# A hybrid decoder step: the turns of q and k placed among retention's phases, and two orders changed on VectorE

## The reference, cut to what matters

```
# stick-breaking attention, a block of queries
z    = (q . k) * d**-0.5
mask = k_pos < q_pos
lm   = where(mask, log_sigmoid(-z), 0)
la   = log_sigmoid(z) + (reverse cumsum of lm over keys) - lm
a    = where(mask, exp(la), 0);   o = a @ v

# retention, a chunk of 128 tokens
att = (q k^T) * inner_decay
o   = att v + (q s) * q_decay
s   = s * chunk_decay + (k * k_decay)^T v
```

## Time and profile before

| | value |
|---|---|
| median of the runs | 1003.06 us |
| profiled execution, its own time | 1003.46 us |
| its span in the profile | 1001.8 us |
| PE busy | 926.3 us (92%) |
| PE weight loads busy | 500.6 us (50%) |
| DVE busy | 477.1 us (48%) |
| ACT busy | 291.1 us (29%) |
| GpSimd busy | 231.7 us (23%) |

### The profile page before, as it was taken

How to read it: one execution, slowest core, us unless ns; L and a number is a source line. 1 busy time by engine, 2 the same in 40 slices (tenths; PEclk the granted TensorE clock), 3 DMA queues, 4 the chain that set the end, 5 groups by cost and what they waited for, 6 DMA issues and landing times.

```text
span 1001.8 us, 15841 instructions
## 1 busy us (share of the span) xinstructions
PE 926.3 (92%) x5202; PEld 500.6 (50%) x5202; DVE 477.1 (48%) x971; ACT 291.1 (29%) x710; POOL 231.7 (23%) x321
## 2 busy tenths in 40 slices
PE   6999999999877978999999999998889898899998
PEld 3544444444444543445465676565544444565444
DVE  1247777879234433112114343724666777556211
ACT  5111111112533334023001010424555556445100
POOL 0000232300123311052243333000443444233000
PEclk9999999999989989999999999999899999999999
DMA  9233666573234327695143132130112132132211
GB/s 346 74 141 118 219 229 227 184 243 71 76 98 138 115 92 223 270 203 186 32 138 121 49 127 55 54 86 11 40 56 64 50 100 94 30 92 71 87 43 43
DMA packets 86070, 117.59 MB, mean 117 GB/s; under 512 B 21006, under 2 KB 49886, under 8 KB 85678
## 3 DMA queue, kind: packets, MB, share of 16 engines
q1 hardware_dynamic: 66432, 80.96, 25.1%
q0 software_dynamic: 9920, 27.31, 9.5%
q10 hardware_dynamic: 9648, 8.41, 2.6%
HBM read 108.68 MB, written 11.36 MB: 120 GB/s over the span
## 4 chain that ended last, share of the span: by engine, by line
PE 86%; DVE 6%; ACT 5%; DMA 2%; issue 1%; SPq 0%; ACTq 0%; DVEq 0%
PE ps L732 25%; PE ps L985 11%; PE ps L991 6%; PE ps L1278 6%; PE ps L1008 4%; PE ps L741 3%; PE ps L1159 3%; PE ps L1170 3%; PE ps L1047 3%; PE ps L928 3%; PE ps L1235 2%; PE ps L908 2%; PE ps L880 2%; PE ps L1025 1%; DVE work L1982 1%
## 5 line engine op out<-in xcount | busy, mean ns | idle before, releaser
L732 PE MATMUL ps<-wring,arena 128*128 128x512 f32 x448 | 197.8, 600 | 1.5 <-issue 1.5
L732 PEld LDWEIGHTS ps<-wring,arena 128*128 128x128 f32 x448 | 85.0, 192 | 105.7 <-issue 105.6
L680 POOL TENSOR_TENSOR z<-z,work 128x1024 f32<-128x1024 f32 (+1 forms) x64 | 80.2, 1252 | 200.8 <-DVE work L1990 200.1
L985 PE MATMUL ps<-wring,z 128*128 128x512 f32 (+2 forms) x320 | 108.4, 494 | 0.0
L1501 ACT ACTIVATE z<-ps,work 128x512 f32<-128x512 f32 (+3 forms) x128 | 66.4, 526 | 71.1 <-DVE work L1982 58.7
L1333 ACT ACTIVATE z<-ps 128x512 f32<-128x512 f32 (+1 forms) x64 | 27.4, 433 | 181.8 <-PE ps L732 147.6
L985 PEld LDWEIGHTS ps<-wring,z 128*128 128x128 f32 x320 | 55.4, 192 | 44.5 <-issue 42.9
L358 POOL DMA_DIRECT2D arena<-cache_sb_k x64 | 34.4, 537 | 165.5 <-DVE work L1618 141.9
L1830 DVE TENSOR_TENSOR arena<-ps,consts 128x512 f32<-128x512 f32 x32 | 30.3, 1022 | 84.0 <-PE ps L1025 84.0
L1512 ACT ACTIVATE arena<-ps 128x512 f32<-128x512 f32 (+3 forms) x128 | 48.9, 438 | 31.2 <-PE ps L1159 31.2
L1982 DVE TENSOR_REDUCE work<-ps 128x1 f32<-128x512 f32 (+3 forms) x128 | 56.9, 486 | 2.2
(11 more groups left out here) (315 smaller groups left out, 1290.7 us busy)
## 6 DMA issues: line engine op xcount, KB each, us to landing
wring<-w_in SPq DMA_DIRECT2D x12, 2048.0 KB, 9.6
arena<-cache_sb_k POOLq DMA_DIRECT2D x64, 256.0 KB, 3.0
arena<-cache_sb_v SPq DMA_DIRECT2D x64, 256.0 KB, 3.4
wring<-w_out SPq DMA_DIRECT2D x3, 2048.0 KB, 7.9
arena<-cache_sel_k SPq DMA_DIRECT2D x64, 64.0 KB, 1.8
consts<-cache_sel_v SPq DMA_DIRECT2D x64, 64.0 KB, 1.8
consts<-aux SPq DMA_DIRECT2D x1, 2299.5 KB, 16.0
xres<-x_prompt SPq DMA_DIRECT2D x4, 512.0 KB, 8.8
```

What stands on the lines that cost most here:

```text
L680: nc.gpsimd.tensor_tensor(P_u(n), P_u(n), bc(coef(n).unsqueeze(2), [P, 2, (NT - n % NT) * P]), ALU.mult).then_inc(n_scaled, 1)
L732: mm = pe.matmul(ps[:, t, 0:width], stat, mov, start=(k == 0), stop=(k == KT - 1))
L985: mm = pe.matmul(ps[:, bank, at:at + w], normed1(k, t), wring[:, slot, k, lo:lo + w], start=(k == 0), stop=(k == KT - 1))
```

## The change

The item list goes. Steps are numbered 0 to 15 and step n uses bank pair n mod 2, so the scores alternate strictly. A turn no longer takes a place in that alternation. The first turn goes into banks 0 and 1 during the last input projection, and DVE copies it as before. The three others are issued at the second step of a pair (n = 1, 5, 9), in banks 4 and 5, which belong to retention: after the tails, PE waits until retention has read these banks, turns, does `values` of the step before and the pages, then waits until the copies are made and only then does retention's phase of that step. ACT makes these copies, after `weights` of the step.

On DVE, the softplus of step n + 1 comes right after `masked` of step n, then `mix`, and then retention's part. On GpSimd, iteration n does the tail sums of step n and no longer those of step n + 1. On ACT, `tail_of` of step 0 comes before the exponential of the sample scores.

```diff
 # PE
-                def front(r):
-                    kind, i, s = sb_items[r]
-                    lo, _ = sb_banks(r)
-                    if r >= 2:
-                        before = sb_items[r - 2][0]
-                        pe.wait_ge(sb_T if before == "turn" else sb_a, sb_count(before, r - 2))
...
+                def sb_turn(i, bank):
+                    for w in range(2):
+                        for t in range(NT):
+                            col = (SQ, SK)[w] * HW + i * P
+                            mm = pe.transpose(ps[:, bank + w, t * P:(t + 1) * P], z[:, t, col:col + P], ident)
+                    mm.then_inc(sb_turned, 1)
+                def front(n):
+                    i, s = SB_STEPS[n]
+                    lo, _ = sb_banks(n)
+                    pe.wait_ge(sb_a, n - 1) if n >= 2 else pe.wait_ge(bank_free, 5 + 5 * RG + NT)
+                    pe.wait_ge(sb_T, 2 * i + 2)
...
+                for n in range(NSTEP):
+                    i, j = n // NT, n % NT
+                    turning = j == 1 and i + 1 < NHP
+                    tails(n)
+                    if n == 0:
+                        rs_sums()
+                    if turning:
+                        pe.wait_ge(*((ret_T, 2), (ret_attm, 4), (ret_S, 4))[i])
+                        sb_turn(i + 1, 4)
+                    else:
+                        retention(n)
+                    if n:
+                        values(n - 1)
+                    sample_pages(n)
+                    if turning:
+                        pe.wait_ge(sb_T, 2 * i + 4)
+                        retention(n)
+                    if n + 2 < NSTEP:
+                        front(n + 2)
 # ACT
-                act.wait_ge(ds_lasum, 1)
-                nc.scalar.activation(zs, zs, ACT.Exp).then_inc(ds_a, 1)
...
+                def sb_copies(i, bank):
+                    act.wait_ge(sb_turned, i + 1)
+                    act.wait_ge(sb_z, NT * (i - 1)) if i > 1 else None
+                    nc.scalar.activation(qT_s(i), ps[:, bank, :], ACT.Copy, scale=SCALE).then_inc(sb_T, 1)
+                    nc.scalar.activation(kT_s(i), ps[:, bank + 1, :], ACT.Copy).then_inc(sb_T, 1)
+                tail_of(0)
+                act.wait_ge(ds_lasum, 1)
+                nc.scalar.activation(zs, zs, ACT.Exp).then_inc(ds_a, 1)
                 tail_of(1)
+                for n in range(NSTEP):
+                    i, j = n // NT, n % NT
+                    weights(n)
+                    if j == 1 and i + 1 < NHP:
+                        sb_copies(i + 1, 4)
+                    retention(n)
+                    if n + 2 < NSTEP:
+                        tail_of(n + 2)
 # DVE
-                    if step:
-                        masked(r)
-                        retention(n)
-                    if r + 2 < NITEM:
-                        softplus(r + 2)
-                    if step and n >= NT and n % NT == 0:
-                        mix(n // NT - 1)
+                    masked(n)
+                    if n + 1 < NSTEP:
+                        softplus(n + 1)
+                    if n >= NT and n % NT == 0:
+                        mix(n // NT - 1)
+                    retention(n)
 # GpSimd
-                    if n + 1 < NHP * NT:
-                        tail_sums(n + 1)
+                    tail_sums(n)
```

More of the change, by code:

```diff
@@ L435, in build, with sb_banks @@
             PTURN_STEPS = {41: 0, 42: 1, 43: 2}
[L437 to L454, removed]
+            SB_STEPS = [(i, s) for i in range(NHP) for s in reversed(range(NT))]
+            NSTEP = len(SB_STEPS)
+            def sb_banks(n):
+                return 2 * (n % 2), 2 * (n % 2) + 2
             @block.sync
@@ L648, in _ @@
                 pool.wait_ge(bank_free, 5 + 5 * NCHUNK0)
-                for n in range(NHP * NT):
-                    if n + 1 < NHP * NT:
-                        tail_sums(n + 1)
+                for n in range(NSTEP):
+                    tail_sums(n)
                     if n < 3 * NT and n % 3 == 0:
@@ L874, in tails @@
-                def tails(r):
-                    _, i, s = sb_items[r]
-                    n, (lo, _), N = sb_step(r), sb_banks(r), (NT - s) * P
+                def sb_turn(i, bank):
[9 more added lines that the diff above has]
+                    pe.wait_ge(sb_T, 2 * i + 2)
+                    for u in range(2):
+                        mm = pe.matmul(ps[:, lo + u, 0:(NT - s) * P], kT_s(i, halves(u))[:, s * P:(s + 1) * P],
+                                       qT_s(i, halves(u))[:, s * P:SEQ], start=True, stop=True)
+                    mm.then_inc(sb_z, 1)
@@ L878, in tails @@
+                def tails(n):
+                    i, s = SB_STEPS[n]
+                    (lo, _), N = sb_banks(n), (NT - s) * P
                     pe.wait_ge(sb_sp, n + 1)
@@ L888, in tails, with values @@
                     mm.then_inc(sb_la, 1)
-                def values(r):
-                    _, i, s = sb_items[r]
-                    pe.wait_ge(sb_a, sb_step(r) + 1)
+                def values(n):
+                    i, s = SB_STEPS[n]
+                    pe.wait_ge(sb_a, n + 1)
                     if s == NT - 1:
@@ L917, in _ @@
                         ds_sums()
-                        front(0)
+                        pe.wait_ge(bank_free, 5 + 5 * RG + 2)
+                        sb_turn(0, 0)
                 project_rows(RG, RG % 2, xnT_ready, 0)
+                front(0)
                 front(1)
@@ L930, in out0_tile @@
                             mm.then_inc(mm_done, 1)
-                done = None
-                for r in range(NITEM):
-                    step = sb_items[r][0] == "step"
-                    if step:
[L936 to L943, removed]
-                    if r + 2 < NITEM:
-                        front(r + 2)
+                for n in range(NSTEP):
[17 more added lines that the diff above has]
+                        front(n + 2)
                 pe.wait_ge(w_loaded[0], 16 * 5)
                 out0_tile(0, range(KT - 1))
-                values(done)
+                values(NSTEP - 1)
                 out0_tile(1, range(KT - 1))
@@ L1392, in retention, with tail_of @@
                         rsqrt(stats[0:NB, 40:48], DH, gn_rstd, NT + 1)
-                def tail_of(r):
-                    _, i, s = sb_items[r]
-                    n, (lo, hi) = sb_step(r), sb_banks(r)
+                def tail_of(n):
+                    i, s = SB_STEPS[n]
+                    lo, hi = sb_banks(n)
                     dst = ln_s(n, s)
@@ L1401, in tail_of, with weights @@
                     softplus_tail(ps[:, lo:hi, 0:(NT - s) * P], dst, sb_ln)
-                def weights(r):
-                    _, i, s = sb_items[r]
-                    n, (lo, hi) = sb_step(r), sb_banks(r)
+                def weights(n):
+                    i, s = SB_STEPS[n]
+                    lo, hi = sb_banks(n)
                     act.wait_ge(sb_masked, n + 1)
@@ L1409, in weights @@
                     nc.scalar.activation(a_s(s), ps[:, lo:hi, 0:(NT - s) * P], ACT.Exp).then_inc(sb_a, 1)
-                tail_of(1)
[L1412 to L1417, removed]
+                def sb_copies(i, bank):
[6 more added lines that the diff above has]
+                nc.scalar.activation(zs, zs, ACT.Exp).then_inc(ds_a, 1)
+                tail_of(1)
+                for n in range(NSTEP):
+                    i, j = n // NT, n % NT
[5 more added lines that the diff above has]
+                        tail_of(n + 2)
                 act.wait_ge(mix_turned, NT + 1)
@@ L1733, in retention, with softplus @@
                         rows_gate()
[L1735 to L1745, removed]
+                def softplus(n):
+                    i, s = SB_STEPS[n]
+                    lo, hi = sb_banks(n)
+                    N = (NT - s) * P
                     dve.wait_ge(sb_ln, n + 1)
@@ L1748, in softplus, with masked @@
                     TT(sp_s(s)[:, :, 0:P], sp_s(s)[:, :, 0:P], bc(cst("strict").unsqueeze(1), [P, 2, P]), ALU.mult).then_inc(sb_sp, 1)
-                def masked(r):
-                    lo, hi = sb_banks(r)
-                    dve.wait_ge(sb_la, sb_step(r) + 1)
+                def masked(n):
+                    lo, hi = sb_banks(n)
+                    dve.wait_ge(sb_la, n + 1)
                     TT(ps[:, lo:hi, 0:P], ps[:, lo:hi, 0:P], bc(cst("strict_neg").unsqueeze(1), [P, 2, P]), ALU.add).then_inc(sb_masked, 1)
@@ L1764, in own_columns @@
                     TT(om[:, b * HW:(b + 1) * HW], ps[:, 7, :], cst("own_head"), ALU.mult).then_inc(ds_om, 1)
[L1766 to L1771, removed]
-                        own_columns(n // 2 - 1)
-                    if step:
-                        masked(r)
-                        retention(n)
-                    if r + 2 < NITEM:
-                        softplus(r + 2)
-                    if step and n >= NT and n % NT == 0:
+                dve.wait_ge(sb_turned, 1)
```

(11 more changed lines are left out.)

## The result

The changed kernel takes 976.71 us, the median of 4 runs (974.5 to 979.01), against 1003.34 for the kernel before: a ratio of 0.9733 (95% interval 0.971 to 0.9757). I had forecast 979.6, within 970 to 989. The profiled execution took 977.28 us with a span of 975.6; before it was 1003.46, so 26.2 us went where 23.9 were forecast.

What follows compares the result with a forecast made beforehand. PE's order of work and its idle places were taken as the bound. Terms -14.4 - 5.3 - 7.6 - 0.6 + 2.7 + 1.3 = -23.9 us took 1003.46 to 979.6 us, range 970 to 989.

Steps and rivals of the forecast that it cites:

- Scores two steps ahead, -14.4: Stick-breaking steps: scores issued two steps ahead cover the chain before the tails, so PE's waits there go, -14.4 us.
- The three stalls: PE's idle times of 4.79, 4.80 and 4.80 us before the tails of a pair's widest step, forecast to go.
- My margin of 0.3 us: Narrowest case, second pair: 5.2 us of PE work against a 4.92 us chain; lateness beyond 0.3 us costs PE in full.
- VectorE's order, -5.3: On DVE, mask ahead of the next softplus and mix ahead of retention end the values matmul's waits for the mix, -5.3 us.
- The clock, -7.6 and +1.3: PE's half-speed work behind five stops goes, -7.6 us; page waits may cause one more slow stretch, +1.3 us.
- The second term: One more 2.5 us stretch at half speed after page waits, +1.3 us, with bounds 0 and 9.3.
- the rival with five falls: The clock falls at page waits, five times 1.85 us instead of one of 1.3: +8.0, 987.6 us; chance 0.07.
- The first step, -0.6: On ACT, step 0's softplus goes ahead of the exponential of the samples, which stood on the chain, -0.6 us.
- Copies and GpSimd, 0: ACT's copies of turned q and k stay hidden; GpSimd's sums come some 2 us before they are needed; cost 0.
- The page ring, +2.7: Four V-page buffers reload late: page waits 16.4 us (turning steps 5.4, opening 5.0), +2.7 us against before.
- The second count: A check of the changed stretch from PE's busy time: 97.7 us of work, 119.1 us instead of 143.9, -24.8 us.
- my slower rival: Tails, mask and softplus form a closed cycle, engines working in series: +6.1 us, 1009.6 us; chance 0.03.

Runs made afterwards that it cites:

- e2: The kernel before with VectorE's new order alone, turns left where they were; 997.08 us, ratio 0.9939.
- e1: The changed kernel with VectorE's old order (mask, retention's part, softplus of step n + 2, then mix); 991.79 us, ratio 0.9887.
- e7: The changed kernel with the mix behind retention's part on VectorE, the mask still ahead of the next softplus; 976.26 us, ratio 0.9731.
- e8: The changed kernel with the mask of step n + 1 behind the softplus of step n + 2, the mix still ahead of retention's part; 986.41 us.
- e3: The changed kernel with the three copies of turned q and k made by VectorE in place of ScalarE; 976.57 us, ratio 0.9747.
- e10: The changed kernel with GpSimd's sums of tails one step ahead of its retention jobs, as before; 976.56 us, ratio 0.9742.
- e4: The changed kernel with seven page buffers in place of four and the page loads written out one by one; 965.35 us, ratio 0.9629.
- e5: The changed kernel with its four page buffers but the page loads written out one by one, a control; 978.24 us, ratio 0.9751.

## Why the prediction was right, step by step

*Scores two steps ahead, -14.4.* Right. The three stalls are gone; they stay in e2, where only VectorE's order is changed, and are gone in e1, where it is not. So the placement removes them. My margin of 0.3 us held.

*VectorE's order, -5.3.* Right in the trace: no values matmul waits for the mix. The reason was half right. I put the mix "behind both", the mask of step n+1 and the softplus of n+2; in the order before it stands behind that softplus and ahead of that mask. e7 and e8 show that this softplus is what counts, and that the mix may stand behind retention.

*The clock, -7.6 and +1.3.* The first is right in place, since one low stretch is left, the one at the start; but it was too small. The rows that I halved end before the clock is back. Taken up to where it is back, the five stretches are these (kernel before, columns as above):

```profile
287.70:292.50 4.80, 4.80 (x9) 2.67 (x10) 0.68 (x2) 0.00 (x0) 0.00 (x0) 0.50 0.00 0
323.50:326.60 3.10, 3.10 (x4) 1.48 (x5) 0.68 (x2) 0.00 (x0) 0.00 (x0) 0.50 0.00 0
343.90:347.10 3.20, 3.20 (x16) 1.17 (x17) 0.76 (x2) 1.88 (x5) 2.73 (x4) 0.50 0.01 3
359.90:364.10 4.20, 4.20 (x8) 2.13 (x9) 0.67 (x2) 0.00 (x0) 0.00 (x0) 0.50 0.02 4
384.60:388.10 3.50, 3.50 (x10) 1.34 (x7) 0.00 (x0) 1.32 (x3) 0.00 (x0) 0.51 0.97 301
```

That is 18.8 us of work, and half of it, an estimate of 9.4 us, was lost. The second term did not come: from the first pages on the clock is at 1.00 (changed kernel),

```profile
266.00:374.50 108.50, 104.56 (x633) 55.78 (x625) 54.45 (x95) 52.50 (x86) 36.39 (x38) 1.00 0.53 167
```

through all page waits, which come in pieces between the matmuls of a group, the longest 1.65 us. So the rival with five falls is out. It is not far off, though: in e7_mix_last one piece of such a wait was 2.31 us long (PE's timeline), and behind it the clock fell (busy time by stretch).

```profile
364.56 1.02 PE L892 MATMUL ps<-arena,work 128*8 128x512 f32 x2 [2.31 <-DMA arena<-cache_sb_v]
```
```profile
365.00:368.40 3.40, 3.16 (x7) 0.31 (x6) 1.67 (x3) 0.41 (x2) 0.00 (x0) 0.59 0.30 100
```

*The first step, -0.6.* Right: from the last projection to the first tails 261.80 - 257.01 = 4.8 us, before 5.35.

*Copies and GpSimd, 0.* Right, by e3 and e10, and the 2 us to spare on GpSimd were 1.9. The copies have nothing to spare: at the second turn the copy of k is made at 300.85, the page matmuls before it end at 300.82, and the chain that ended last runs through the copy (in order of time):

```profile
300.35 0.50 ACT xres L1404
300.89 0.49 PE ps L807 x2
```

*The page ring, +2.7.* Right: 16.4 us of page waits forecast, 17.1 measured by the line's account, and e4 with e5 shows that it is buffers coming back late and not the rate. The shares are near too. Counted from PE's timeline, as the time of a group beyond 0.97 us, the turning steps have 4.6 us (5.4 forecast), the opening steps 5.3 (5.0), the last three steps 6.2 (5.0). The largest single wait, 4.8 us, is in the step before the last, beside the load of the output weights, where I had 3.2.

*The sum* was 2.3 us too small: 23.9 forecast, 26.2 measured in the profiled execution. The low clock makes 1.8 of it (9.4 for 7.6) and the second fall that did not come 1.3; the pages took 0.7 more. That gives 26.3. The second count had a slip: it took all 9.3 us of page waits out of PE's busy time, but 1.0 of them was idle time already (kernel before):

```profile
PE ps L908 <- DMA arena<-cache_sb_v: 1.0, 2, 0.6
```

With 8.3 in its place and 9.4 for the clock the work is 114.6 - 9.4 - 8.3 = 96.9 us. In the changed kernel it is 96.8 (110.09 busy less the 13.3 of page waits that stand within it), so PE's work is the same before and after, as forecast. My 97.7 was near because the two slips partly cancel. The cycle of tails, mask and softplus, my slower rival, never closed: the tails wait for a softplus only at the start.

## What to carry to other kernels

A stall that another engine's queue order causes is partly hidden as long as a larger one stands beside it: take the larger away alone and the next comes out bigger than it was (15.8 us against 9.7), so try such edits together before judging either. In an engine's queue, put what is ready now, and what frees a buffer, ahead of what waits for a step further on. Before predicting that stalls vanish, ask which ring of buffers had used those stalls to refill, work out its turnaround, and subtract.

## What the runs showed of the hardware that I had not expected

With VectorE's old order the granted clock was at 0.52 for 10.2 us in a row (301.8 to 312.0), behind a stop of 2.43 us, and PE was busy for 10.16 of them. In the kernel before, behind a stop of 4.79 us, it was at 0.50 for 4.8 us of work (287.7 to 292.5). So the longer stop did not have the longer low stretch behind it.

Nor does the length of a single stop tell whether the clock falls. In e1_dve_old it fell behind a stop of 1.74 us,

```profile
317.94 1.04 PE L892 MATMUL ps<-arena,work 128*8 128x512 f32 x8 [1.74 <-DVE arena L1758]
```
```profile
319.20:322.70 3.50, 3.50 (x8) 1.73 (x9) 1.08 (x2) 2.25 (x7) 2.16 (x2) 0.51 0.62 196
```

and in e5_ring4 it stayed at 1.00 behind one of 2.19:

```profile
368.77 3.67 PE L907 MATMUL ps<-arena,work 128*8 128x512 f32 x8 [2.19 <-DMA arena<-cache_sb_v]
```
```profile
368.80:372.40 3.60, 3.52 (x9) 0.38 (x9) 2.16 (x4) 0.42 (x2) 0.00 (x0) 1.00 0.82 263
```

What decides it stays open. That the clock held through the changed kernel's page waits is what its trace shows, and nothing that these runs let one count on.
